# A fused two-block transformer on one core: the values of even and odd heads of the second attention go to two PSUM banks, and the turned outputs to two halves of the second bank

## The reference

```
o_cmp = softmax(q kc^T + bias) vc          # compressed keys, 31 of them
o_slc = softmax(q k_slc^T + bias) v_slc    # selected key blocks
o_win = softmax(q k_win^T + bias) v_win    # window of 512 keys
o     = gates[0]*o_cmp + gates[1]*o_slc + gates[2]*o_win
return o.reshape(B, S, 1024) @ w_o
```

## Time and profile before

| | |
|---|---|
| median of 3 runs | 2069.5 us (2066.62 to 2070.35) |
| the profiled execution's own time | 2069.23 us |
| its span in the trace | 2067.4 us |
| mean granted clock of TensorE | 0.978 |
| TensorE busy, share of the span | 95% |
| VectorE, ScalarE, GpSimd busy | 47%, 41%, 39% |
| the stage of the change | about 664 to 867 us |

### The profile page before, as it was taken

The page is one execution under the profiler, slowest core; times in us unless marked ns, Lnnn a source line. Parts: engine busy times, 40 slices in busy tenths (PEclk is TensorE's granted clock), DMA queues, the critical chain, the costliest instruction groups (busy, mean ns, idle before and its releaser), DMA issues.

```text
span 2067.4 us, 29274 instructions
## 1 busy us (share of the span) xinstructions
PE 1963.5 (95%) x9688; PEld 1637.3 (79%) x9688; DVE 969.7 (47%) x2281; ACT 839.3 (41%) x1520; POOL 813.4 (39%) x390
## 2 busy tenths in 40 slices
PE   8999999999988999999999998999999799999996
PEld 5897888888777888878888887877888588787784
DVE  5555655221536766546553214566511544545414
ACT  4564222232443766542222233332222356565523
POOL 3533554444363000125444443445544134343340
PEclk9999999999998989999999999999999999999998
DMA  7532554232242112025443222222222121111221
GB/s 250 156 105 96 189 174 163 99 102 92 84 148 79 47 46 61 27 81 199 167 172 111 92 101 82 95 98 98 91 100 94 41 82 62 61 61 62 67 76 41
DMA packets 70027, 209.56 MB, mean 101 GB/s; under 512 B 9739, under 2 KB 15115, under 8 KB 69948
## 3 DMA queue, kind: packets, MB, share of 16 engines
q1 hardware_dynamic: 57724, 174.72, 25.4%
q10 hardware_dynamic: 12224, 33.85, 5.0%
HBM read 196.90 MB, written 8.49 MB: 99 GB/s over the span
## 4 chain that ended last, share of the span: by engine, by line
PE 62%; issue 21%; POOL 9%; DVE 6%; ACT 2%; POOLq 0%; DVEq 0%; ACTq 0%
PE bank L963 16%; PE bank L965 15%; PE bank L964 15%; POOL wsp L446 9%; PE bank L1261 3%; PE bank L1234 1%; PE bank L1245 1%; PE bank L1419 1%; PE bank L1129 1%; PE bank L1438 1%; PE bank L1017 1%; PE bank L1106 1%; PE bank L1257 1%; PE bank L1430 1%; PE bank L1117 1%
## 5 line engine op out<-in xcount | busy, mean ns | idle before, releaser
L446 POOL TENSOR_TENSOR wsp<-raw,wsp 128x1024 fp32r<-128x1024 f32 x294 | 729.0, 2485 | 1009.8 <-ACT wsp L539 1009.6
L963 PE MATMUL bank<-xs,wsp 128*128 128x512 f32 x1320 | 521.5, 395 | 19.1 <-issue 8.4
L964 PE MATMUL bank<-xs,wsp 128*128 128x512 f32 x1320 | 516.5, 391 | 0.0
L965 PE MATMUL bank<-xs,wsp 128*128 128x512 f32 x1320 | 516.4, 391 | 0.0
L539 ACT ACTIVATE wsp<-raw 128x1024 fp32r<-128x1024 f32 x294 | 307.5, 1052 | 234.6 <-PE bank L965 207.6
L963 PEld LDWEIGHTS bank<-xs,wsp 128*128 128x128 f32 x1320 | 249.6, 189 | 76.2 <-issue 15.0
L963 PE MATMUL bank<-xk,wsp 128*128 128x512 f32 x752 | 294.2, 391 | 9.6 <-DVE xk L1544 5.1
L964 PE MATMUL bank<-xk,wsp 128*128 128x512 f32 x752 | 293.5, 390 | 0.0
L965 PE MATMUL bank<-xk,wsp 128*128 128x512 f32 x752 | 293.3, 390 | 0.0
L965 PEld LDWEIGHTS bank<-xs,wsp 128*128 128x128 f32 x1320 | 249.3, 189 | 52.6
L964 PEld LDWEIGHTS bank<-xs,wsp 128*128 128x128 f32 x1320 | 249.5, 189 | 51.4 <-issue 1.0
(11 more groups left out here) (297 smaller groups left out, 2450.2 us busy)
## 6 DMA issues: line engine op xcount, KB each, us to landing
raw<-weights SPq DMA_DIRECT2D x294, 512.0 KB, 3.5
gen<-ada ACTq DMA_DIRECT2D x48, 512.0 KB, 3.5
tmp<-mid SPq DMA_DIRECT2D x64, 128.0 KB, 2.9
bias_b<-bias_row ACTq DMA_DIRECT2D x1, 4096.0 KB, 37.0
mid<-bias_b SPq DMA_DIRECT2D x8, 512.0 KB, 3.9
hT<-xT SPq DMA_DIRECT2D x2, 1024.0 KB, 9.5
bias_a<-bias_row ACTq DMA_DIRECT2D x1, 2048.0 KB, 16.5
mid<-bias_a SPq DMA_DIRECT2D x8, 256.0 KB, 2.9
```

Source lines behind the costliest of these rows:

```text
L446: pool.tensor_tensor(wsp[:, slot, 1, :], raw[:, slot, :], wsp[:, slot, 0, :].bitcast(F32), ALU.subtract).then_inc(w_ready, 1)
L963: pe.matmul(dst, w[0], x[0], start=first, stop=False)
L964: pe.matmul(dst, w[0], x[1], start=False, stop=False)
L965: return pe.matmul(dst, w[1], x[0], start=False, stop=last)
```

## The change

The value products of odd units go to `bank[7]`, those of even units stay in `bank[6]`. The turned outputs get 256 columns of `bank[7]`, from 192 on, beside the values: blocks 0 and 2 in the first 128, blocks 1 and 3 in the second. `b_keep` therefore runs twice in a half, after units 3 and 7, with 256 columns each. The wait of `b_values` goes from the unit before to the one two back; odd units of blocks 0 and 2 wait for a `b_keep` instead. The wait of `b_turn_out` for an emptied bank goes. The semaphore `b_den` is dropped and its count is carried by `b_fac`.

```diff
+TURNED = 192
@@ TensorE, b_values
-                if again(i, m, 1):
-                    pe.wait_ge(b_o_ready, i * 16 + m)
-                dst = bank[6]
+                if again(i, m):
+                    pe.wait_ge(b_o_ready, i * 16 + (m - 1))
+                if e and blk == 0:
+                    pe.wait_ge(mid_ready, i * 2 + (MID_B + pp))
+                if e and blk == 2:
+                    pe.wait_ge(b_kept, i * 2 + (pp + 1))
+                dst = bank[6 + e]
@@ TensorE, b_turn_out
                 pe.wait_ge(b_o_ready, i * 16 + (m + 1))
-                if blk == 0:
-                    pe.wait_ge(mid_ready, i * 2 + (MID_B + pp))
-                pe.transpose(bank[7][:, blk * P:blk * P + P], b_o[blk % 2], ident[:, :]).then_inc(b_ot, 1)
+                at = TURNED + blk % 2 * P
+                pe.transpose(bank[7][:, at:at + P], b_o[blk % 2], ident[:, :]).then_inc(b_ot, 1)
@@ VectorE, b_norm
-                dve.reciprocal(stat[:, b, 8:10], stat[:, b, 4:6]).then_inc(b_den, 1)
-                dve.wait_ge(b_den, i * 16 + (m + 1))
+                dve.reciprocal(stat[:, b, 8:10], stat[:, b, 4:6]).then_inc(b_fac, 1)
+                dve.wait_ge(b_fac, i * 32 + (2 * m + 1))
@@ VectorE, b_outputs
-                dve.wait_ge(b_fac, i * 16 + (m + 1))
+                dve.wait_ge(b_fac, i * 32 + (2 * m + 2))
-                src = bank[6]
+                src = bank[6 + e]
@@ VectorE, b_keep
-                if m % 8 == 7:
-                    dve.wait_ge(b_ot, i * 8 + 4 * (m // 8) + 4)
-                    dve.tensor_copy(mid[:, i * 2 + m // 8, :], bank[7][:, :]).then_inc(mid_ready, 1)
+                if m % 4 == 3:
+                    half = m % 8 // 4
+                    dve.wait_ge(b_ot, i * 8 + (m // 2 + 1))
+                    dve.tensor_copy(mid[:, i * 2 + m // 8, 256 * half:256 * half + 256], bank[7][:, TURNED:TURNED + 256]
+                                    ).then_inc(mid_ready if half else b_kept, 1)
```

More of the change, by code:

```diff
@@ L271, in build @@
                                                  sem("b_pt_ready"))
-        b_den, b_fac, b_pv, b_part, b_o_ready, b_ot = (sem("b_den"), sem("b_fac"), sem("b_pv"), sem("b_part"),
+        b_kept, b_fac, b_pv, b_part, b_o_ready, b_ot = (sem("b_kept"), sem("b_fac"), sem("b_pv"), sem("b_part"),
                                                        sem("b_o_ready"), sem("b_ot"))
```

## The result

| | before | after |
|---|---|---|
| median, us | 2068.06 (4 runs) | 2045.91 (2044.9 to 2046.63, 4 runs) |
| span of the profiled execution | 2067.4 | 2043.0 |
| mean granted clock | 0.978 | 0.988 |

The ratio is 0.989, with a 95% interval of 0.9879 to 0.9902: 22.2 us faster. The forecast was 2051.0, its range 2046 to 2060.

The account below looks back on a forecast made before the run. TensorE, busy 95% of the span, was taken as the bound, losing time to idling and low clock. Regular halves 6.0, jumps 11.5 and end 0.7 sum to 18.2 us off 2069.2: 2051.0 us, range 2046 to 2060.

Parts of the forecast that it names:

- The ring through bank 6: Value matmuls and VectorE's output operations wait on each other through one bank; TensorE waits 20 times, 13.4 us in all.
- The regular halves: Stretches between starts of unit 2's values, 22.62 us each: 0.86 us less per half, 6.0 us over seven.
- the stops removed: TensorE's stops ahead of the values of units 7, 0 and 2: 0.44 + 0.58 + 1.07 = 2.09 us per half.
- the new wait of unit 1: Unit 1's values wait for the copy of turned outputs after unit 7, queued on VectorE behind unit 0's outputs: 1.00 us.
- that of unit 5: Unit 5's values wait for the copy after unit 3, behind unit 4's outputs on VectorE: 0.23 us.
- The jumps: Two halves where the hardware loop jumps back: excess of 12.5 us shrinks to 1.0 as the clock holds, 11.5 us gained.
- forecast stop of 0.5 us: At each jump back TensorE idles about 0.5 us at the transpose of unit 5's outputs, not 2.41 us.
- The end: Last unit's values lose their 0.94 us wait, unit 13 pays 0.23: 0.7 us gained, the clock assumed to fall anyway.
- the rivals (2047): Clock holds at the end of the stage too: some 4 us more gained, 2047 us; chance 0.06.
- the slower rival: Clock falls at unit 1 in each half, after a 1.0 us stop amid transposes: 2072 to 2084, say 2078 us; chance 0.06.
- the rule on transposes: Transposes don't count as busy TensorE like matmuls, so a stop amid them at unit 1 would likelier cost the clock.
- The copy isn't dear: Rival on VectorE's copies: 0.69 us for 256 columns, each new wait 0.27 longer, 3.8 us in seven halves, 2054.8; chance 0.07.

Follow-up runs that it names:

- The experiment at unit 6: Changed kernel with the old wait (for the outputs of the unit before) put back in unit 6 alone of 16: 2060.6 us, ratio 0.9963.
- the version with the copies early on ScalarE: Changed kernel with both copies moved from VectorE to ScalarE, one ahead of its slot's exponentials, the projection's first input ahead of the last copy: 2039.2 us, ratio 0.9853.

## Why the prediction was right in direction and short by 4 us

- **The ring through bank 6.** Right. Putting the wait back in every unit brings back the old time to 0.05%.
- **The regular halves.** Forecast 0.86 us per half, measured 1.10. The terms: 2.09 for the stops removed measured 0.38 + 0.52 + 1.07 = 1.97; the new wait of unit 1, 1.00, measured 0.92; that of unit 5, 0.23, measured 0.15 (0.49 at unit 13 of the last iteration); the copy, taken as 0.42, takes 0.42. Together 1.97 - 0.92 - 0.15 = 0.90. The last 0.2 us are a term that I hadn't: values that are released only when TensorE is already there take longer to get under way. Those of unit 7 take 0.27 us from L1257 to L1261 in the earlier trace rows (713.58 to 713.85), and 0.16 in the changed kernel without the stop (711.43 to 711.59). Units 7, 0 and 2 gained 0.1 us each in this way, and unit 5 lost 0.05. Unit 1 lost nothing: it took 0.28 before the change too, when unit 0's outputs ended at 718.77 and its values started at 718.83, so that its distance of 0.78 "without a wait" was one that just ended in time.
- **The jumps.** The mechanism is right: unit 6 goes ahead, the transpose of unit 5's outputs waits instead, and the clock holds. The forecast stop of 0.5 us measured 0.78 and 0.82, and each such half is 1.0 us longer than a regular one. VectorE's first pause was 0.16 us shorter at the first jump and its second 0.39 longer (0.76 to 1.15), so that the outputs came 0.23 us later than I reckoned. 10.4 us in place of 11.5. The experiment at unit 6 shows that the clock's fall hangs on this stop.
- **The end: the step that failed.** "The clock falls there in any case, I assume." In one profile of the changed kernel it doesn't fall, in the other it is low for 3.4 us in place of 10.2. I had costed the stop of 0.94 us at its own length, 0.7 us net, and kept the clock out of it, though at the jumps I had counted that a fall costs more than the stop before it. Measured in place of 0.7: up to the start of the last unit's values 1.26 us (14.35 to 13.09), although unit 13 waits 0.49 us and not 0.23; from there to the projection 1.74 (5.58 to 3.84), nearly all of it the matmuls that had run at the lower clock (3.62 to 1.95); and behind the projection's start another 2.4 us of low clock in one profile. In the other the two stretches to the projection gain the same 3.0 us in all, and behind it about 1.1, since the clock was low for 2.7 us there. This was among the rivals (2047), with a chance of 0.06, as if it excluded the main case; it comes on top of it. That the stop ahead of the last unit makes the low clock longer is borne out by the last column of the table (6.8 to 10.2 us in all five kernels that have it, 0 to 3.4 in eight of the nine others); the run that puts back this stop alone points the same way, but its time isn't clear of the noise.
- **The other rivals.** The clock doesn't fall at unit 1 (the stop is 0.8 us, and no half of the changed kernel has a low clock), so that neither the slower rival nor the rule on transposes shows here. The copy isn't dear: 16 of them take 0.41 to 0.42 us each. That the stop of unit 1 is there because of the order on VectorE, and could go, is shown by the version with the copies early on ScalarE.

What stays open: why a stop of 1.74 us left the clock alone and one of 1.63 didn't, and why the end had 0 us of low clock in one execution of the changed kernel and 3.4 in another. What makes VectorE pause at the jump is open too, and with it how long the pause will be in a given loop.

## What to carry to other kernels

Where two engines hand one bank back and forth, don't only add up the stops: look at where the partner engine has a hiccup of its own, because the tight wait passes it on in full, and here TensorE then paid a second time in clock. It can be worth taking the hiccup away first: writing VectorE's loop out gave the kernel before 13 us, and the changed one only 2. More than half of this change's gain lay at two jumps back and at the end, in a stage that looked like a steady pipeline.

When a wait replaces another, read what stands ahead of the awaited instruction in its own queue. Here moving the copy to another engine brought 1.4 us; only when two orders had been mended did it bring 7.

## What the runs showed of the hardware that wasn't expected

- A loop's jump back cost VectorE 2.6 to 2.8 us in most versions, 0.3 us or less with the four copies out of the body, and 3.9 to 4.0 us with four memsets of 0.06 us and their waits in their place. TensorE crossed its own jump without a gap.
- After a stop of 2.4 to 3.0 us of TensorE the granted clock was at 0.50 (1.2 GHz) for 10.2 to 13.7 us in all six cases with VectorE's loop and the old wait at the jump. After stops of 0.6 to 1.0 us at the jumps of the other versions it never fell in a profile, and of two stops of 1.6 to 1.7 us one was followed by a fall.
